# Two gate-and-up projections with seven half-size products in place of eight

## The reference

```python
def swiglu_ffn(h, w_gu, w_dn):
    gate, up = jnp.split(h @ w_gu, 2, axis=-1)
    return (jax.nn.silu(gate) * up) @ w_dn
...
def conv_ffn(h, w_up, conv_w, conv_b, w_down):
    u = h @ w_up
    s = u.shape[1]
    up_pad = jnp.pad(u, ((0, 0), (CONV_WIDTH - 1, 0), (0, 0)))
    uc = conv_b + sum(conv_w[i] * up_pad[:, i:i + s] for i in range(CONV_WIDTH))
    gate, val = jnp.split(uc, 2, axis=-1)
    return (jax.nn.silu(gate) * val) @ w_down
```

## Time and profile before

| what | value |
|---|---|
| three runs | 3288.94, 3290.53, 3292.64 us; median 3290.53 |
| profiled execution, first to last instruction (span) | 3285.9 us; its time with what lies around it is not given apart |
| PE busy | 3116.8 us, 95% of the span, 18680 matmuls |
| weight loads busy | 2442.2 us, 74%, beside the matmuls |
| DVE, ACT, POOL busy | 1452.4, 1054.4 and 376.7 us (44%, 32%, 11%) |
| chain that ended last | PE 85%, DVE 8%, ACT 4% |
| read from HBM, written | 161.63 MB and 17.96 MB |

### The profile page before, as it was taken

How to read it: one execution, slowest core, us unless ns; L and a number is a source line. 1 busy time by engine, 2 the same in 40 slices (tenths; PEclk the granted TensorE clock), 3 DMA queues, 4 the chain that set the end, 5 groups by cost and what they waited for, 6 DMA issues and landing times.

```text
span 3285.9 us, 42656 instructions
## 1 busy us (share of the span) xinstructions
PE 3116.8 (95%) x18680; PEld 2442.2 (74%) x18680; DVE 1452.4 (44%) x2104; ACT 1054.4 (32%) x1616; POOL 376.7 (11%) x392
## 2 busy tenths in 40 slices
PE   6999999998999999999998989988889999999999
PEld 2479866666768888888886767766667888888887
DVE  6268626666344111113337253266653443434333
ACT  4245424443233111112124654344433322222111
POOL 1023203343212000000003000021112000000000
PEclk9999999999899999999999989999989999999999
DMA  6012200000041111112112101000022111111212
GB/s 249 32 65 91 94 26 13 26 14 13 15 168 61 52 52 52 39 45 90 52 61 81 61 26 39 6 6 3 2 104 80 49 52 52 43 47 39 99 45 75
DMA packets 35209, 182.33 MB, mean 55 GB/s; under 512 B 4261, under 2 KB 4261, under 8 KB 21584
## 3 DMA queue, kind: packets, MB, share of 16 engines
q1 hardware_dynamic: 22176, 133.18, 11.5%
q0 software_dynamic: 12848, 46.43, 3.7%
HBM read 161.63 MB, written 17.96 MB: 55 GB/s over the span
## 4 chain that ended last, share of the span: by engine, by line
PE 85%; DVE 8%; ACT 4%; DMA 1%; issue 1%; POOL 1%; POOLq 0%; DVEq 0%; ACTq 0%; SPq 0%
PE ps L548 18%; PE ps L549 18%; PE ps L550 18%; PE ps L538 9%; PE ps L687 4%; PE ps L751 3%; PE ps L592 2%; PE ps L1228 2%; DMA ar<-in_xT 1%; PE ps L651 1%; PE ps L1089 1%; PE ps L834 1%; PE ps L609 1%; ACT ar L1449 1%; PE ps L1370 1%
## 5 line engine op out<-in xcount | busy, mean ns | idle before, releaser
L548 PE MATMUL ps<-r,r 128*128 128x512 f32 x2632 | 1034.7, 393 | 10.7 <-DVE r L2085 5.4
L549 PE MATMUL ps<-r,r 128*128 128x512 f32 x2632 | 1026.4, 390 | 0.0
L550 PE MATMUL ps<-r,r 128*128 128x512 f32 x2632 | 1026.0, 390 | 0.0
L548 PEld LDWEIGHTS ps<-r,r 128*128 128x128 f32 x2632 | 495.2, 188 | 125.8 <-issue 16.2
L549 PEld LDWEIGHTS ps<-r,r 128*128 128x128 f32 x2632 | 495.4, 188 | 104.6 <-issue 3.0
L550 PEld LDWEIGHTS ps<-r,r 128*128 128x128 f32 x2632 | 495.2, 188 | 103.7
L2078 DVE TENSOR_TENSOR r<-ar,r 128x1024 fp32r<-128x1024 f32 (+1 forms) x170 | 204.6, 1204 | 324.5 <-ACT r L1411 324.4
L1411 ACT ACTIVATE r<-ar 128x1024 fp32r<-128x1024 f32 (+1 forms) x170 | 174.4, 1033 | 534.8 <-PE ps L550 495.4
L1449 ACT ACTIVATE ar<-ps 128x256 f32<-128x256 f32 (+3 forms) x330 | 147.0, 470 | 525.6 <-PE ps L538 117.0
L538 PE MATMUL ps<-ar 128*128 128x128 f32 (+4 forms) x1460 | 242.9, 338 | 3.7 <-ACT ar L1449 3.0
L538 PEld LDWEIGHTS ps<-ar 128*128 128x128 f32 (+1 forms) x1460 | 191.0, 186 | 48.5 <-issue 31.8
(11 more groups left out here) (296 smaller groups left out, 3587.2 us busy)
## 6 DMA issues: line engine op xcount, KB each, us to landing
ar<-in_w_mod SPq DMA_DIRECT2D x24, 1024.0 KB, 4.9
ar<-in_w_gu SPq DMA_DIRECT2D x22, 1024.0 KB, 4.8
ar<-in_w_up SPq DMA_DIRECT2D x22, 1024.0 KB, 4.8
ar<-in_w_in SPq DMA_DIRECT2D x19, 1024.0 KB, 4.8
ar<-in_w_dn SPq DMA_DIRECT2D x32, 512.0 KB, 3.5
x<-ar POOLq DMA_DIRECT2D x48, 256.0 KB, 2.4
ar<-x POOLq DMA_DIRECT2D x24, 512.0 KB, 8.5
ar<-in_xT POOLq DMA_DIRECT2D x16, 512.0 KB, 13.6
```

Source lines behind the costliest of these rows:

```text
L548: M.matmul(o, whk, hi[k][:, a:a + n], start=k == 0, stop=False)
L549: M.matmul(o, whk, lo_[k][:, a:a + n], start=False, stop=False)
L550: ins = M.matmul(o, wlk, hi[k][:, a:a + n], start=False, stop=k == nk - 1)
```

## The change

The product of a weight tile (gate rows a11, a12 and up rows a21, a22, each 128 columns x 512 features) with h (four quarters of 512 features x 512 tokens, x11 to x22) is made with Strassen's algorithm in Winograd's form: seven products of half size (`op` 1 to 7), each 4 k x 3 matmuls, in place of eight. One loop, `gate_up(tag)`, replaces `up_1` and `up_2` on each engine. It walks a list `SEQ`: for each pair of columns m0, m1 the products 1, 2, 6, 5, 7, 4, 3, each for m0 and then m1. Every (op, m) is a unit q, with ten buffers for its weights (`wunits`); their high and low parts are made `LEAD` = 8 units ahead.

- Sums of weights: POOL makes four a tile (`weight_sums`), in place in the ring slot, and for product 6 in the unit's buffer, which it may write when the unit ten places earlier is done.
- Sums of activations: DVE makes t1 to t4 from the quarters, for four feature tiles j, in `second_norm`; each is then split like h (`FACTOR`).
- Partial results: products 1, 6, 7 and 4 add into one bank ("chain"), and ACT copies it out after 1, 6 and 7 (states s1, s2, s3) before the next product adds to it. DVE adds product 2 to s1 (c11, gate, first tokens), 5 to s3 (c22, up, second tokens), 3 to s2 (c12), and c21 is the chain's end. In the first block DVE and POOL then multiply; in the second ACT applies the last tap (`up_taps`, `gate_taps`), DVE the others from SBUF (`conv`), ACT silu, and POOL the product (`act_done`).
- The finished tile goes to HBM (`acts`, 512 KB a tile), and comes back for `down`: the first eight in token halves, then the rest; x comes back in 16 pieces. `down`'s first part takes two output tiles before it turns to the second token half (`DN0`).

```diff
+    SEQ = [(op, m) for m0 in range(0, 22, 2) for op in (1, 2, 6, 5, 7, 4, 3) for m in (m0, m0 + 1)]
+    PLACE = {om: q for q, om in enumerate(SEQ)}
+    NU, LEAD = 10, 8
...
+    def before_unit(tag, q):
+
+        if q >= NU:
+            return product, ("gu", tag, *SEQ[q - NU])
...
+        def gate_up(tag):
+            CHAIN, PAIR = (0, 1, 6), (4, 5, 7)
...
+                else:
+                    pe.wait_ge(*a_evac.at(({6: "s1", 7: "s2", 4: "s3"}[op], tag, m)))
+                    o = bank(("chain", tag, m))
+                xh, xl = FACTOR[op]
+                for j in range(4):
+                    if m == 0:
+                        pe.wait_ge(*v_lo.at(("t", tag, op, j)))
+                    c = slice(128 * j, 128 * j + 128)
+                    M.matmul(o, hi[:, c], xh[j], start=begins and j == 0, stop=False, skip_group_check=True)
+                    M.matmul(o, hi[:, c], xl[j], start=False, stop=False, skip_group_check=True)
+                    ins = M.matmul(o, lo_[:, c], xh[j], start=False, stop=j == 3, skip_group_check=True)
+                ins.then_inc(*product(key))
...
+        def first_state(tag, m):
...
+                if m > 1:
+                    act.wait_ge(*v_evac.at(("conv", m - 2, 0)))
+                state("s1", 1, 2, m, raw_g[m % 2][:, 0:512])
...
+                if 14 <= q + LEAD < len(SEQ):
+                    unit_high(tag, q + LEAD)
+                if op == 1 and m > 1:
+                    first_state(tag, m)
+                elif op == 6 and m > 1:
+                    second_state(tag, m)
+                elif op == 7:
+                    third_state(tag, m)
...
+            if op == 6:
+                dve.wait_ge(*p_wsum.at((3, tag, m)))
+            V.tensor_tensor(lo_, raw_ if op == 6 else slot(name, WCOL[op], 512), hi.bitcast(F32),
+                            ALU.subtract).then_inc(*v_lo(("u", tag, q)))
+            if op == 3:
+                releases(name, (v_lo, ("u", tag, q)))
...
+                        norm(j, 512)
+                        norm(4 + j, 512)
+                        dve.wait_ge(*v_norm.last())
+                        less(x11, x12, None, False, x11, v_step, ("t1", tag, j))
+                        dve.wait_ge(*v_step.last())
+                        less(t2[j], x22, mcol(3, 4 + j), shift, x11, v_step, ("t2", tag, j))
+                    if j:
+                        low_factor(tag, 6, j - 1, t2[j - 1])
...
+                if tag == 2 and op == 1 and m > 1:
+                    gate_conv(m - 2)
+                elif tag == 2 and op == 3:
+                    conv(m, 1, made_2[m % 2], raw_u[m % 2])
...
+            if tag == 2:
+                gate_conv(20)
+                gate_conv(21)
+            split(("dn", tag, 0, 1))
...
+            G.tensor_tensor(a11, a11, a21, ALU.subtract).then_inc(*p_wsum((7, tag, m)))
+            s, k = before_unit(tag, q)
+            pool.wait_ge(*s.at(k))
+            pool.wait_ge(*p_wsum.at((7, tag, m)))
+            G.tensor_tensor(raw_, a22, a11, ALU.subtract).then_inc(*p_wsum((6, tag, m)))
+            G.tensor_tensor(a21, a21, a22, ALU.add).then_inc(*p_wsum((5, tag, m)))
+            pool.wait_ge(*v_lo.at(("u", tag, PLACE[2, m])))
+            pool.wait_ge(*p_wsum.at((6, tag, m)))
+            G.tensor_tensor(a12, a12, raw_, ALU.subtract).then_inc(*p_wsum((3, tag, m)))
...
+            G.dma_start(D["acts"][128 * m:128 * m + 128, :], x).then_inc(*act_out[m % n]((tag, m)))
...
+            for q, (op, m) in enumerate(SEQ):
+                if q + 9 < len(SEQ) and SEQ[q + 9][0] == 6:
+                    weight_sums(tag, SEQ[q + 9][1])
+                if op == (6 if tag == 1 else 5) and m > 1:
+                    act_done(tag, m - 2)
```

More of the change, by code:

```diff
@@ L889, in out_projection @@
                         half_sum(("tail", tag, 0), acc_t, sq_t[1])
[L891 to L944, removed]
@@ L955, in block @@
                      ("dnr", tag, part) if m == 7 and a else None).then_inc(*product(key))
-            for part in range(3 if tag == 2 else 2):
+            for m, a in DN0:
+                block(0, m, a)
+            for part in range(1, 3 if tag == 2 else 2):
                 for m in range(8):
@@ L1705, in out_projection @@
                 split(("wo", tag, m))
[L1706 to L1721, removed]
-                    A.activation(hhi[k][:, a:a + 512], hxt[k][:, a:a + 512], ACT.Identity,
-                                 bias=mcol(3, k) if shift else 0.0).then_inc(*a_hi((("h", tag), k, a)))
@@ new lines, in out_projection @@
+            act.wait_ge(*product.at(("sums", "tail", tag, 0)))
+            for k in range(8):
+                act.wait_ge(*v_res.at(("wo", tag, k, 512)))
+                half_squares(("tail", tag, 512), k, hxt[k][:, 512:1024], sq_t, acc_t)
+                if k in (4, 5, 6):
+                    unit_high(tag, 2 * k - 6)
+                    unit_high(tag, 2 * k - 5)
+            first_state(tag, 0)
+            half_roots(("tail", tag, 512), rb_t)
+            first_state(tag, 1)
+            act.wait_ge(*product.at(("wo", tag, 7, 512)))
@@ L1792, in down @@
                     if m < 7:
-                        split(("dn", tag, part, m + 1))
+                        if part or m:
+                            split(("dn", tag, part, m + 1))
                     elif part < 2:
@@ L2513, in down, with first_residual @@
         def down(tag, gate):
-            for part in range(3):
+            def first_residual(m, a):
+                dve.wait_ge(*(hx_in if a else tile_in)[m].at(("act", tag, m)))
+                residual(("dn", tag, 0, m, a), m, a, gate(m))
+            act_low(tag, 0, 512)
+            for m, a in DN0:
+                if a and m == 1:
+                    split(("dn", tag, 0, 2))
+                elif a == 0 and 1 < m < 7:
+                    split(("dn", tag, 0, m + 1))
+                elif a == 0 and m == 7:
+                    split(("dn", tag, 1, 0))
+                if (m, a) == (7, 512):
+                    act_low(tag, 1, 0)
+                first_residual(m, a)
+            for part in range(1, 3):
                 act_low(tag, part, 512)
@@ L2993, in block @@
+        def block(tag, x_from, saved):
             for k in range(8):
```

455 lines of the change are left out of this document (321 added, 134 removed).

## The result

| | before | after |
|---|---|---|
| runs beside each other | 3289.74 us (3286.1 to 3292.64, 4 runs) | 3256.52 us (3254.76 to 3257.41, 4 runs) |
| span of the profiled execution | 3285.9 | 3255.6 |
| PE, DVE, ACT, POOL busy | 3116.8, 1452.4, 1054.4, 376.7 | 3017.3, 1711.5, 1232.1, 766.2 |

The account below looks back on a forecast made before the run. PE's own pace was taken to bound the two gate-and-up stages. Removed matmuls -119.6, starts +45.6, second middle +20 and end +9 make -45.0: 3290.5 to 3245 us, range 3200 to 3285.

Parts of the forecast that it names:

- Removed: Both gate-and-up stages: 1848 of 2112 matmuls a block stay, 0.2266 us each; 119.6 us go if PE never waits.
- The starts: Start of each gate-and-up stage: PE waits before product 6 and, behind tile 3's fetch, before product 4; 22.8 us each.
- The first middle: First block's gate-and-up stage after its start: nothing closes a loop on PE, 0 us lost.
- The second middle: Second block's gate-and-up stage after its start: a loop through buffers runs 2.2 us a pair over PE's pace; 20 us.
- The forecast's loop: Second block, from product 7 of m0 over POOL's sums, DVE's convolutions, ACT's first-state copy to PE: 38.4 us without port.
- upper bound of 46: High case of the second middle: 5.1 us a pair, POOL additions at 1.50 and five DVE operations 0.3 longer.
- The port: Port shared by DVE and POOL, second block: three DVE lows beside POOL's seven additions slow down, 1.9 us a pair.
- Rival C: Slower than before: POOL's seven sums and DVE work wait for each other; 3336 us at the longest row; chance 0.10.
- The end: End of second block: down's second weight split comes late behind ACT and DVE; 7.1 idle, 1.9 half clock, 9 us.
- Costed at nothing: Extra highs and lows on ACT and DVE, activation stores and loads, POOL's early weight sums: no cost to PE.
- Rival A: PE stays fed: the loop has slack and the fourth tile comes in time; 3204 us, chance 0.12.

Follow-up runs that it names:

- Early units: On the changed kernel, weight parts of units 8 to 13 made ahead of activation sums t3 and t4 at both stage starts; 3249.34 us (0.9882).
- the run that lays it bare: On the changed kernel, DVE instead of POOL multiplies the second block's activations (act_done's product, columns 0 to 19); 3237.86 us (0.9849).
- End split: On the changed kernel, down's second weight tile and second-half activations split ahead of the last gate taps, gate convolutions and silu, second block; 3238.99 us (0.9856).
- the last version: On the three cures together, second block's low and high parts of m1's product 6 made later, high parts at the starts moved; 3212.58 us (0.9777).
- the three cures together: On the changed kernel, earlier split at the second block's end, activations multiplied on DVE there, units 8 to 13 split earlier at both starts; 3216.14 us (0.9789).

## Why the prediction was right, and where it was not

- **Removed, 119.6**: right. The first middle shows it bare: PE 389.0 busy of 389.0, no wait.
- **The starts, 22.8 each**: right, by its steps. The first stage lost 442.5 - 420.5 = 22.0, of it 15.1 in waits (three for product 6's parts, 3.8, 1.7 and 1.8, and 7.7 before product 4), the rest mostly at the lower clock. Product 7 ended at 41.2 (forecast about 40), s3 was copied at 48.7 (49.9), the pair ended at 61.7 (62.7). Two terms were mis-sized: the long wait was 7.7, not ten, and the lower clock cost more than 1.9, since it came behind product 6's waits as well. That they nearly cancel is luck. Early units show the cause: with the fetch released earlier the long wait is 0.7.
- **The first middle, 0**: right.
- **The second middle, 20**: the step that failed. The second stage lost 472.1 - 420.5 = 51.6; counted from the start of product 4 in the first pair it takes 424.2 against the first block's 393.6, so the middle cost 30.6. The forecast's loop exists, and its sum without the port, 38.4, stands beside 38.8 to 39.1 in the run that lays it bare. But a longer one lay over it, which the prediction did not look for because it called the fetch hidden ("the next tile's fetch has two units of slack", written of the first block and carried over). In the second block the low part that releases the slot stands behind DVE's gate convolutions and c11s, and the fetch is a link of a chain that never asks PE. The sign that it gave, one PE wait of 2 to 3 us a pair ended by the first-state copy, was about right in size (1.4 to 2.5) and right in line, and wrong in place: that one is 0.4, and the larger one is the third state. That the upper bound of 46 covers 30.6 is luck: it was made from slower operations in the loop that the forecast knew.
- **The port, 1.9 a pair**: present, but elsewhere and larger: the two low parts beside act_done lose some 4 us a pair, two more beside the sums 1.2 (1.42 and 1.19 us for 0.69). Of the sums on POOL three in four stay near 1.3, the others take 1.5 to 1.76, a few of them above the 1.6 that the prediction named as a sign against it. (The POOL instruction beside the earlier trace rows's first group is a product, not an addition.) Rival C had POOL's sums as the place. Keeping act_done clear of the low parts gave 2 us, as the loop has a second branch over POOL; taking the product off POOL gave 21.
- **The end, 9**: the mechanism was right, its size off: 10.6 of wait instead of 7.1, and 11.9 in the stage, some of it clock; End split gives 11.6 of it back. DVE's last convolution took 3.36 us instead of 1.28 and the split 2.53 instead of 1.2, each beside a product of POOL; these 3.4 us are nearly all that the forecast lacked:

```profile
3006.04 2.33 POOL L3192 TENSOR_TENSOR ar<-ar 128x1024 f32<-128x1024 f32 x1 [5.47 <-ACT ar L1841]
3006.10 3.36 DVE L2633 SCALAR_TENSOR_TENSOR ar<-ar 128x1022 f32<-128x1022 f32 x1
...
3010.63 2.34 POOL L3192 TENSOR_TENSOR ar<-ar 128x1024 f32<-128x1024 f32 x1 [1.27 <-ACT ar L1841]
3011.52 2.53 DVE L2184 TENSOR_TENSOR r<-ar,r 128x1024 fp32r<-128x1024 f32 x1 [2.07 <-ACT r L1434]
```

- **Costed at nothing**: the stores and loads did not stop down. But two weight fetches go out 0.6 us apart in the second block now: the first, a link of loop L, takes 4.7 to 6.2 us to landing, the second 6.6 to 8.3 (the page's 6.4 is the median of both), where each took about 4.8 before. A store of 512 KB ends beside nearly all of the first ones; whether that slows them no run shows.

By stages 119.6 - 22.0 - 51.6 - 11.9 is 34.1, and 33.2 was measured between the medians. Forecast and result lie 12 us apart, 9 of it in the second gate-and-up stage (51.6 for 42.8), 3 in the end. Rival A (3204) is what the last version comes near to, after five edits.

## What to carry to other kernels

When engines feed one another through buffers, write down every loop that closes, also those that leave out the bottleneck engine, with the buffer's release and the transfer as links; the longest period sets the pace, and a wait's releaser only names the place where it comes to light. Cutting one link helps until the next branch or the next loop, so after each cut measure the period, not the wait: here 41.4, then 38.8 to 39.1, then 38.4, with PE's own 38.1 not quite reached. A short list on an in-order engine is moved with its partner: a low part that is put later gains nothing while its high part still stands in the way on the other engine.

## What the hardware showed that was not expected

The granted clock of a stage that no edit touches can differ enough to hide a gain. From the first down's token sums to the second gate-and-up stage the changed kernel and the experiments took 815.4 to 823.5 us: 820.6 to 823.5 in the four with early units, 815.4 to 820.0 in the others. In the windowed attention, changed kernel first, then the three cures together, two equally long windows that begin at the same instruction stand beside another clock (the one before the DMA share):

```profile
1871.01:1904.01 33.00, 24.59 (x142) 17.89 (x142) 14.12 (x19) 20.97 (x56) 0.00 (x0) 0.97 0.09 32
```

```profile
1853.52:1886.52 33.00, 27.50 (x132) 19.87 (x130) 12.35 (x17) 18.42 (x50) 0.00 (x0) 0.84 0.09 32
```

Over the whole stretch the granted clock is 0.95 in each of the four and 0.96 in each of the others, so the edit is likely to bring it about; how stays open, and there is one profiled execution of each. With the 8.8 us by which the first stage's start moves, it can be why sums of single gains miss the medians by some microseconds in both directions.
